# Row numbers for the expert turns: 0/1 matrix products, or lists scattered to memory and read back

## What is computed

```python
_, top_e = lax.top_k(sel, TOP_K)                       # 8 of 64 experts per token
wts = jnp.take_along_axis(scores, top_e, axis=-1)
wts = wts / jnp.sum(wts, axis=-1, keepdims=True) * ROUTED_SCALE
...
def body(y, b):
    rows = lax.dynamic_slice_in_dim(tok_buf, b * MOE_BLOCK, MOE_BLOCK)
    wb = lax.dynamic_slice_in_dim(w_buf, b * MOE_BLOCK, MOE_BLOCK)
    e = block_e[b]
    xb = x_pad[rows]
    hb = jax.nn.silu(xb @ w_gate[e]) * (xb @ w_up[e])
    return y.at[rows].add((hb @ w_down[e]) * wb[:, None]), None
```

## Time and profile before

| what | value |
|---|---|
| three runs | 2834.76, 2837.86, 2840.95 us, median 2837.86 |
| the profiled execution | 2834.48 us, its span 2832.7 us |
| mean granted TensorE clock | 0.978 |
| busy in the span | PE 94%, DVE 66%, ACT 50%, POOL 18% |
| experts' stage, layer 0 and 1 | about 760 to 1590 and 1950 to 2785 us |
| matmuls of `gate_up` and `down` on ring tiles alone, of `index` | busy 699.4, 355.8, 51.9 us |
| row gathers and adds on POOL | 144 each, 977 and 1586 ns median in layer 0 |

### The profile page before, as it was taken

One profiled execution on the slowest core, in us unless ns is written; L12 is line 12 of the kernel. 1 busy time (PEld: TensorE's weight loads), 2 busy tenths in 40 slices (PEclk: granted clock), 3 DMA queues, 4 the chain that ended last, 5 costly groups with the idle time before them and its releaser, 6 DMA issues. The chain is left out here.

```text
span 2832.7 us, 40293 instructions
## 1 busy us (share of the span) xinstructions
PE 2671.8 (94%) x13974; PEld 1212.0 (43%) x13975; DVE 1864.6 (66%) x3373; ACT 1429.0 (50%) x3340; POOL 501.7 (18%) x404
## 2 busy tenths in 40 slices
PE   7998999899899999999999698997999999999994
PEld 3444666445333443434433264443333334333332
DVE  4996555576667666666665555766666667677655
ACT  1113555332166666666665241332656666666653
POOL 0000000111022222222222121100222222222212
PEclk9999999999999999999999799998999999999997
DMA  9777300201499999999999622016999999999996
GB/s 363 261 269 208 141 16 9 81 30 45 181 363 346 331 320 349 362 353 345 377 336 325 221 103 88 30 45 261 328 311 357 320 376 350 345 377 295 334 338 208
DMA packets 147093, 714.98 MB, mean 252 GB/s; under 512 B 16702, under 2 KB 22078, under 8 KB 94665
## 3 DMA queue, kind: packets, MB, share of 16 engines
q1 hardware_dynamic: 104252, 556.14, 50.1%
q0 software_dynamic: 42336, 154.16, 21.2%
q10 hardware_dynamic: 304, 2.11, 0.2%
HBM read 597.50 MB, written 114.84 MB: 251 GB/s over the span
## 5 line engine op out<-in xcount | busy, mean ns | idle before, releaser
L1692 ACT ACTIVATE xT<-xt_blocks 32x256 f32<-32x256 f32 x2208 | 913.9, 414 | 42.6 <-DVE xt_blocks L1559 14.8
L1771 PE MATMUL exG<-ring,xT 128*32 128x512 f32 (+2 forms) x2352 | 699.4, 597 | 2.9 <-DMA ring<-in_exp_w_up_dram 2.4
L1771 PEld LDWEIGHTS exG<-ring,xT 128*32 128x32 f32 (+2 forms) x2352 | 231.9, 141 | 308.0 <-issue 303.9
L1805 PE MATMUL exD<-ring,ex_hT 128*32 128x512 f32 (+2 forms) x1176 | 355.8, 606 | 2.4 <-DVE w_o L1597 1.2
L1564 DVE TENSOR_SCALAR ex_e<-ex_e 128x256 f32<-128x256 f32 x142 | 43.4, 306 | 426.9 <-ACT ex_e L1704 426.6
L1565 DVE RECIPROCAL ex_e<-ex_e 128x256 f32<-128x256 f32 x142 | 248.9, 1753 | 4.9
L1704 ACT ACTIVATE ex_e<-exG 128x256 f32<-128x256 f32 x142 | 54.4, 383 | 315.0 <-PE exG L1771 315.0
L1771 PE MATMUL exG<-oT,xT 128*32 128x512 f32 (+2 forms) x592 | 197.8, 600 | 1.0 <-DVE xT L1553 1.0
L1771 PE MATMUL exG<-w_fnet,xT 128*32 128x512 f32 (+2 forms) x608 | 176.7, 600 | 2.4 <-DMA ring<-in_exp_w_up_dram 2.4
L1523 DVE TENSOR_TENSOR mod<-place,slots 128x1024 bf16<-128x1024 f32 (+3 forms) x196 | 174.1, 912 | 4.5 <-PEq L234 3.6
L1805 PEld LDWEIGHTS exD<-ring,ex_hT 128*32 128x32 f32 (+2 forms) x1176 | 116.4, 142 | 128.7 <-issue 127.8
(11 more groups left out here) (424 smaller groups left out, 4319.2 us busy)
## 6 DMA issues: line engine op xcount, KB each, us to landing
ring<-in_exp_w_gate_dram SPq DMA_DIRECT2D x64, 1024.0 KB, 10.8
ring<-in_exp_w_up_dram SPq DMA_DIRECT2D x64, 1024.0 KB, 14.9
ring<-in_exp_w_down_dram SPq DMA_DIRECT2D x64, 1024.0 KB, 9.2
ada_w<-in_w_ada_dram SPq DMA_DIRECT2D x48, 512.0 KB, 5.6
oT<-in_exp_w_gate_dram SPq DMA_DIRECT2D x17, 1024.0 KB, 9.9
oT<-in_exp_w_up_dram SPq DMA_DIRECT2D x17, 1024.0 KB, 13.9
oT<-in_exp_w_down_dram SPq DMA_DIRECT2D x17, 1024.0 KB, 9.3
fT<-in_exp_w_gate_dram SPq DMA_DIRECT2D x17, 1024.0 KB, 10.4
```

Of the source, the lines that this page charges most:

```text
L1692: last = act.activation(xT[m * UNIT:(m + 1) * UNIT, par, :, a * UNIT:(a + 1) * UNIT], parts[a * UNIT:(a + 1) * UNIT, m], ACT.Copy)
L1771: last = pe.matmul(psG[par][p:p + m], xT[:, par, k, p:p + m], ring[s % RING][:, 0:2, k * FF:(k + 1) * FF], start=k == 0, stop=k == KT - 1)
L1805: last = pe.matmul(psD[p:p + m, c], hT[:, k * P + p:k * P + p + m], ring[s % RING][:, 2, k * D + c * 512:k * D + (c + 1) * 512], start=k = ...
```

## The change

The rows, sums' rows and weights of turns 20 to 70 no longer come from index products. For each token (128 partitions x 8 groups) the DVE makes, out of `place`, the eight slots (turn and row in it) where the token is worked on, and its weight for each. POOL scatters these 8192 entries of two numbers (the token's number, the weight) to a DRAM tensor `list_scratch` laid out by row and turn, with 64 indirect DMAs of 128 entries, and reads the lists of all turns back with one DMA. The first 64 places of a row of that tensor take the entries that have no slot. Before that SP fills the turns' part of both layers' tensors with dummy rows. Turns 0 to 19 and the overflow round keep their matrices and products.

On the engines, in each layer:

- `onehot`, `index`, `indices` and `targets` of turns 20 to 70 fall away; semaphore counts go through `nth`.
- DVE gets `slot_keys` in iteration 1, `slot_rows` in 2, `slot_weights` in 3 to 10, and `slot_lists` in 15, ahead of `hidden`(15). `overflow` moves from iteration 9 to 17. One 128x512 copy stands in the router stage behind `idx_done`.
- POOL gets two iotas, the sends in iterations 4 to 13 (6 or 7 each) behind `add`, and in iteration 14 the read of the lists. Gathers of turns 20 on wait for `list_ready`.
- SP gets two loads at the stage's head, and waits for `list_ready` before what it fetches early at s = 40.

```diff
+def list_constants():
+
+    f = np.float32
+    p = np.arange(P)
+    base, upper, empty = [], [], []
+    for layer in range(DEPTH):
+        turns, _, _ = schedule(layer)
+        at, half = np.zeros(EXPERTS, f), np.zeros((P, len(turns)), f)
+        for b, turn in enumerate(turns):
+            for i, (_, r, done, row, n) in enumerate(turn):
+                if done == 0:
+                    at[r] = (b + SENDS) * P + row
+                half[row:row + n, b] = i
+        none = np.zeros((P, len(turns), 2), f)
+        none[:, :, 0] = DUMMY + p[:, None]
+        base.append(at)
+        upper.append(half)
+        empty.append(none.reshape(P, -1))
+    return {"list_base": np.stack(base), "list_half": np.stack(upper), "list_empty": np.stack(empty)}
...
+                        for l in range(DEPTH):
+                            sp.dma_start(list_dram[l][:, SENDS:].rearrange("p t c -> p (t c)"), A["list_empty"][l]).then_inc(emptied, 16)
...
+                        dve.tensor_copy(mod[:, 3 * D:3 * D + NT * E].rearrange("p (t e) -> p t e", e=E), psM[:, :, E:])
...
+                LIST, SEND_FROM, SEND_IN = 20, 4, 10
...
+                def nth(b):
+
+                    return b if isinstance(b, int) and b < LIST else b - T + LIST
...
+                        sp.dma_start(base, A["list_base"][layer:layer + 1].to_broadcast([P, E])).then_inc(base_in, 16)
+                        sp.dma_start(half, A["list_half"][layer]).then_inc(half_in, 16)
...
                             if s == 40:
                                 sp.wait_ge(yo_out[0], 16 * (NT // 2))
+                                sp.wait_ge(list_ready, 2)
                                 fetch_early(sp, layer)
...
+                        def send(first_entry, last_entry):
+
+                            for c in range(first_entry, last_entry):
+                                t, j = divmod(c, TOP_K)
+                                pool.wait_ge(entries_done, t + 1)
+                                if c == 0:
+                                    pool.wait_ge(numbered, 2)
+                                    pool.wait_ge(emptied, 16 * DEPTH)
+                                pool.indirect_dma_start(out=list_dram[layer].rearrange("p t c -> (p t) c"),
+                                                        out_offset=bass.IndirectOffsetOnAxis(ap=slot_at[:, c:c + 1], axis=0),
+                                                        in_=entries[:, t, j], in_offset=None).then_inc(listed, 16)
...
-                            pool.wait_ge(idx_done, b + 1)
+                            listed_row = isinstance(b, int) and LIST <= b < T
+                            if listed_row:
+                                pool.wait_ge(list_ready, 2)
+                            else:
+                                pool.wait_ge(idx_done, nth(b) + 1)
                             rows_read(pool, b - lag)
                             if not isinstance(b, int):
                                 settle(pool, waited)
+                            at = row_at[:, b:b + 1] if listed_row else idx[:, par:par + 1]
...
+                            i = b - SEND_FROM
+                            if 0 <= i < SEND_IN:
+                                send(SENDS * i // SEND_IN, SENDS * (i + 1) // SEND_IN)
+                            if i == SEND_IN:
+                                pool.wait_ge(listed, 16 * SENDS)
+                                pool.dma_start(spare[:, 512:512 + 2 * T], list_dram[layer][:, SENDS:].rearrange("p t c -> p (t c)")
+                                               ).then_inc(list_in, 16)
...
+                            by = lists[:, b, 1:2] if LIST <= b < T else w_all[:, ds(b, 1)]
...
+                        def slot_keys():
+
+                            dve.wait_ge(caps_in, 16)
+                            dve.wait_ge(base_in, 16)
+                            wide = lambda a: a.unsqueeze(1).to_broadcast([P, NT, E])
+                            list_link(dve.tensor_tensor(part, place[:], wide(caps[:]), ALU.is_lt))
+                            list_link(dve.scalar_tensor_tensor(out=part, in0=place[:], scalar=0.0, in1=part, op0=ALU.is_ge, op1=ALU.mult))
+                            list_link(dve.tensor_tensor(key, place[:], wide(base), ALU.add))
+                            list_link(dve.tensor_tensor(key, key, part, ALU.mult))
...
+                        def slot_rows():
+
+                            for t in range(NT):
+                                last = dve.max(slot8[:, t], key[:, t])
+                            list_link(last)
+                            keys8 = slot8.rearrange("p t j -> p (t j)")
+                            dve.wait_ge(numbered, 2)
+                            list_link(dve.tensor_tensor(keys8, keys8, nowhere, ALU.max))
+                            list_link(dve.tensor_copy(slot_at, keys8))
...
+                        def slot_weights(t):
+
+                            for j in range(TOP_K):
+                                last = dve.scalar_tensor_tensor(out=part[:, j], in0=key[:, t], scalar=slot8[:, t, j:j + 1], in1=wts[:, t],
+                                                                op0=ALU.is_equal, op1=ALU.mult)
+                            list_link(last)
+                            list_link(dve.tensor_reduce(entries[:, t, :, 1], part, AX, ALU.add))
+                            dve.sem_inc(entries_done, 1)
+
+                        def slot_lists():
+
+                            dve.wait_ge(list_in, 16)
+                            dve.wait_ge(half_in, 16)
+                            dve.tensor_copy(row_at, lists[:, :, 0]).then_inc(list_ready, 1)
+                            dve.scalar_tensor_tensor(out=sum_at, in0=lists[:, :, 0], scalar=2.0, in1=half, op0=ALU.mult, op1=ALU.add
+                                                     ).then_inc(list_ready, 1)
...
-                            if b == 9:
+                            if b == 17:
                                 overflow()
-                            if b + AHEAD < T:
+                            if b + AHEAD < LIST:
                                 onehot(b + AHEAD, par)
                             elif b + AHEAD == T:
                                 dve.wait_ge(table_in, 16)
                                 onehot_over(T, 0, 2)
                             if b + 2 < T:
                                 turn_blocks(b + 2, par)
+                            if b == 1:
+                                slot_keys()
+                            elif b == 2:
+                                slot_rows()
+                            elif b < NT + 3:
+                                slot_weights(b - 3)
+                            elif b == SEND_FROM + SEND_IN + 1:
+                                slot_lists()
                             hidden(b, par, 2)
                             if b + 1 == T:
                                 rows(T, 1 - par, 2)
-                            if b + AHEAD <= T:
+                            if b + AHEAD < LIST or b + AHEAD == T:
                                 indices(b + AHEAD, par, 2)
-                            targets(b - 1, 1 - par, max(0, b - 2) * 16)
+                            if b - 1 < LIST:
+                                targets(b - 1, 1 - par, max(0, b - 2) * 16)
                             weigh(b - 1, 1 - par, max(0, b - 2) * 16)
...
-                            if b + AHEAD < T:
+                            if b + AHEAD < LIST:
                                 index(b + AHEAD, par)
```

More of the change, by code:

```diff
@@ L209, in trunk @@
     row_dram = dram("row_scratch", [2, 2 * D])
+    list_dram = [dram(f"list_scratch{l}", [P, SENDS + len(schedule(l)[0]), 2]) for l in range(DEPTH)]
     table_dram = dram("table_scratch", [BLOCKS, 4], I32)
@@ L1415, in experts @@
                 HAND, AHEAD, SPLIT, Q = 2, 4, 5, P // UNIT
+                LIST, SEND_FROM, SEND_IN = 20, 4, 10
+                spare = mod[:, 3 * D:5 * D]
+                wts = spare[:, 0:512].rearrange("p (t e) -> p t e", e=E)
+                key = spare[:, 512:1024].rearrange("p (t e) -> p t e", e=E)
+                part = spare[:, 1024:1536].rearrange("p (t e) -> p t e", e=E)
+                slot8 = spare[:, 1536:1600].rearrange("p (t j) -> p t j", j=TOP_K)
+                slot_at = spare[:, 1600:1664].bitcast(U32)
+                line, rank8 = spare[:, 1664:1728], spare[:, 1728:1792]
+                entries = spare[:, 1792:1920].rearrange("p (t j c) -> p t j c", j=TOP_K, c=2)
+                base, nowhere, half = spare[:, 1920:1984], spare[:, 1984:2048], mod[:, D:D + T]
+                lists = spare[:, 512:512 + 2 * T].rearrange("p (t c) -> p t c", c=2)
+                row_at, sum_at = (mod[:, 3 * D + 768 + i * P:3 * D + 768 + i * P + T].bitcast(U32) for i in range(2))
+                base_in, half_in, list_own, entries_done, listed, list_in, list_ready, numbered = (sem(n) for n in (
```

(16 more changed lines are left out.)

24 lines of the change are left out of this document (15 added, 9 removed).

## The result

| kernel | median of runs | lowest to highest | profiled execution |
|---|---|---|---|
| before | 2838.11 us (6 runs) | 2834.76 to 2840.95 | 2834.48 us |
| changed | 2867.42 us (6 runs) | 2854.93 to 2877.55 | 2861.46 us |

The ratio is 1.0105, 95% interval [1.0087, 1.0122]: 29.3 us slower, where +10.2 was forecast (2848, range 2800 to 2885). The direction is right and the time lies in the range. Both have to be understood.

The account below looks back on a forecast made before the run. PE was taken to bound the kernel, the weight stream next. Stalls of +50.4 us for two layers, with -28.6 - 11.1 - 2.4 + 1.4 + 0.5, gave +10.2: 2848 us on the median, range 2800 to 2885.

Parts of the forecast that it names:

- rival E: POOL late as forecast, but the list's read overtakes the adds: no change, 2837 us; chance 0.18.
- Index products, -28.6: PE, turns 20 to 70: 102 index products removed at 0.28 us each, all on the path, -28.6 us.
- `overflow`, -11.1: `overflow` leaves iteration 9, where PE waits for the matrix behind it: 5.0 and 6.1 us saved, -11.1.
- Weights of turn 15, layer 1, -2.4: PE's 2.35 us wait for weights there goes when PE comes later than now by more than that.
- Sends, 7.1 and 2 of clock per layer: POOL's send turns take 12.7 us against PE's 11.05; late gathers stall PE 7.1 us per layer, plus 2 of clock.
- The list, 14.1 and 2 of clock per layer: The list lands just behind the add; `slot_lists`, ahead of `hidden`(15), stalls PE 14.1 us per layer, plus 2 of clock.
- DVE's slot work, 0: Keys, slots and weights in iterations 1 to 10, some 2.5 to 2.8 us each, covered by DVE's idle time: cost 0.
- The copies and loads, +1.4 and +0.5: One 128x512 copy per layer ahead of the experts, +1.4 us; SP's loads, two DRAM copies and issue slots, +0.5.
- A: Sends take 0.94 us with no lock, POOL keeps pace, PE never waits for gathers: 2813 us; chance 0.24.
- B: A send costs `add`'s 1.59 us because it, too, writes DRAM: 2917 us; chance 0.06.
- C: Sends that start first hold up DVE's small products by some 0.5 us each: about +32, 2880 us; chance 0.05.
- D: Weight stream at its limit: the 28.6 us come back as waits for `ring`, 2876 us; chance 0.05.

Follow-up runs that it names:

- second measurement: The changed kernel measured again with no edit, in another loading and on another chip than the first time: 2833.3 us, ratio to before 0.9991.
- Late list: Changed kernel with lists used from turn 28, `slot_lists` only in iteration 23 and `overflow` at 25: 2814.7 us, ratio to before 0.9913.
- best: Changed kernel with lists used from turn 32, four sends per turn over 16 iterations, `slot_lists` in 26, `overflow` at 29: 2809.5 us, ratio to before 0.9911.

## Why the prediction was right, and where it was wrong

The forecast names a loss, and the first measurement shows one, but for another reason; that it came so near is luck.

**The step that failed** is the sum's silent assumption that a send costs POOL time and nothing else. In the first measurement the send turns took 138.5 and 144.7 us against 117.5 and 111.1 of the same code without gaps: 55 us in the two layers, of which the wait for the list gives 26 back (43.0 and 47.0 against 55.9 and 59.9), since the DVE reaches it later. No term and no rival had PE slowed by sends. The idle time under "issue" is 25.6 us; the rest of the loss is not in these lines (matmuls that are recorded as drawn out, and a granted clock of 0.64 in the stretch where PE stopped and started). So 2848 lies nearer to 2867 than its working deserves: without the gaps the sum should have come to -3.3 instead of +10.2, the difference of the profiled executions of the second measurement and of before (2831.18 and 2834.48). That is the outcome of rival E, no change, by other sizes.

Step by step, in that second measurement, by PE's turns:

- *Index products, -28.6*: -25.5. The 50 turns from 20 to 70 take 11.2 and 11.3 us less, and 45 of them lose a product: 0.25 each, where 0.28 was taken from the turns of 32 small products.
- *`overflow`, -11.1*: right for its own turns. Turns 3 to 13 take 117.1 and 117.1 before and 111.9 and 110.9 without sends: 11.4.
- *Weights of turn 15, layer 1, -2.4*: wrong in sign. It was to go if PE came later than before. But PE comes earlier: `overflow` gave it 6.2 us, and in this layer the sends took nothing. Turn 13 to 14 takes 19.3 against 13.6: +5.7. Every kernel that has `overflow` out of iteration 9 and no gaps pays here (16.8 without sends, 17.9 in "best"); with `overflow` at 9 it is 11.6. So much of `overflow`'s gain in layer 1 comes back as a wait for weights, a link between two terms that the sum treats as separate.
- *Sends, 7.1 and 2 of clock per layer*: 2.2 and 0. The pace was nearly right: a turn of POOL of 12.4 against 12.7. Its parts were not: a send takes 0.96 us, 1.26 with the gap (1.35 taken); the DVE holds sends up for some 0.2 a turn in layer 0 (0.9 taken); and `add` stands some 0.8 a turn in layer 0 for the landing of an earlier one, directly or through `targets`, for which the forecast had nothing. In layer 0 the first gather behind sends came 6 us late (841.45), because `add` had waited for a landing; 6 + 9 x 1.36 - 12.2 = 6.0. In layer 1 it came about 1 late (2029.65), and 9 x 1.24 more, 12.2 in all, just reach the tolerance of 12.2. "Late list", where no wait for the list hides it, shows these sizes: turns 3 to 20 take 196.6 and 196.0 there, 189.7 and 195.3 in "best", 6.9 and 0.7 more. In the changed kernel only 2.2 of the 6.9 come ahead of the list's wait; the rest falls together with it, where the sum has them one behind the other.
- *The list, 14.1 and 2 of clock per layer*: 38.6 - 22.1 = 16.5 and 30.6 - 21.8 = 8.8. In layer 0 idle time and clock are as forecast: PE idles 14.2, and the turn behind it is 2.1 longer. In layer 1 PE idles only 6.6, since it comes later by the wait for weights. In layer 0 the list landed just behind the add, as taken. The Trainium skill's fixed 2 us ("SBUF — State Buffer", section "The DMA setup-cost knee") isn't seen under this load: 4.9 to 11.5 us in the two executions shown.
- *DVE's slot work, 0*: right, by the run without sends.
- *The copies and loads, +1.4 and +0.5*: not taken apart. The terms above give -25.5 - 11.4 + 5.7 + 2.2 + 16.5 + 8.8 = -3.7, the profiled executions -3.3, so little is left for them.

Of the rivals, A (POOL keeps pace) comes true with 4 sends a turn, not with 6.4, though the sends' own price is nearly A's. B is out: a send takes 0.96 with a DRAM target, so it is the accumulation or the size that makes `add` 1.59. C is out: the 128 small products of `slot_weights`, most of them beside sends, take 242 to 285 ns each in the first measurement and up to 334 in the second, median 0.28; C wanted 0.5 us more for each. Of the lock that the Trainium skill describes ("SBUF — State Buffer", section "Who interferes with whom") the runs show again the half in which POOL waits, sends of up to 1.86 us as in the earlier trace rows, and not the other. D is out: the turns got shorter at a DMA share of 1.02 to 1.03; only turn 15 of layer 1 pays something of the kind.

What stays open is how sends slow PE, and, strictly, whether it is the sends: the kernel without them was in no job with gaps. Shown is: before, which has no sends, stayed at 2837 to 2838 in every job; the versions with sends had the gaps in some jobs and not in others; in the one job where three versions had them, turns 3 to 13 of both layers took, over twice the 111 of a stage free of them, 67 us more with 6.4 sends per turn (7 of it is in the second measurement too), 39 with 5.8 and 10 with 4 (`overflow`'s 11 taken off); and PE's small groups of products stand 0.5 us apart. That could be the supply of PE's instructions. But ACT or DVE, too, starts late behind a product of PE that the trace has as done ("remote") in all five traces with gaps, and in none of the nine others, while POOL's sends keep their 1.26 us; so something slow in PE's signals, or in how its work ends, is as likely. No view shows the cause, and no run told one from the other.

## What to carry to other kernels

A chain of small DMAs on an in-order queue is priced by its pace against the bottleneck's turn and by the lateness which the buffers behind it allow; below that pace it is free, above it everything that stands behind it is late. A wait for its result belongs as late on the waiting engine as its consumer allows: moving this one was worth 13 to 22 us, nearly as much as the 102 products bring (25). Two waits in the same turns are not two terms of a sum: here a stall taken away made the next wait, for weights, longer, and a stall put back (`overflow` at 9) cost 2 us instead of 11. Time on the engine that bounds the kernel is read on that engine's timeline. And a difference of 1% wants a second job before it is explained.

## What the runs showed that I had not expected

PE can run an unbroken row of matmuls 40 times slower (12.2 us for 0.29) with nothing in the waits, in some jobs with a program that sends many small scatters; runs within a job agree (2829.5 to 2842.8, and 2868.6 to 2883.9), so their interval does not cover it. A direct read of 71 KB landed 4.9 and 9.2 us after issue in one execution and 5.6 and 11.5 in another, with the adds of its queue. DVE operations of 128x64 take 0.28 us each in a row of eight independent ones, against 0.23 for the one in the earlier trace rows, which waits for the one before; what makes the difference, no run shows.
